# Delta rule: half of the state products and of the next key product between the levels, and a first copy of every second column

## The reference, cut to what matters

```
A   = -beta_t * (K K^T) * decay, below the diagonal      (128 x 128)
T   = (I - A)^-1                                         by doubling, levels 1 to 6
Z   = V - exp(g) * (K S)                                 S: state before the chunk
U   = beta * (T Z)
O   = exp(g) * (Q S)  +  ((Q K^T) * decay) U
S'  = exp(g_end) * S + K^T (U * decay to the end)
```

## Time and profile before

| | us |
|---|---|
| median of 3 runs | 2904.25 |
| the profiled execution | 2905.02 |
| its span | 2902.9 |
| delta stage, first to last level (1459.2 to 1913.0) | 453.8 |
| TensorE busy in that stretch | 444.44 |

### The profile page before, as it was taken

How to read it: one execution, slowest core, us unless ns; L and a number is a source line. 1 busy time by engine, 2 the same in 40 slices (tenths; PEclk the granted TensorE clock), 3 DMA queues, 4 the chain that set the end, 5 groups by cost and what they waited for, 6 DMA issues and landing times.

```text
span 2902.9 us, 43802 instructions
## 1 busy us (share of the span) xinstructions
PE 2729.6 (94%) x16708; PEld 2265.2 (78%) x16708; DVE 1647.1 (57%) x2847; ACT 1177.6 (41%) x2145; POOL 370.2 (13%) x583
## 2 busy tenths in 40 slices
PE   6999899998898997999999999999999998988899
PEld 4756777777757996887688888877777787977899
DVE  4565533334665666885377777773433345468565
ACT  4343422223534445346344455552422234343443
POOL 0000000000000000000066666640000000023000
PEclk9999999999999998999999999999999999999999
DMA  7263244442363553223200000032444433210453
GB/s 281 87 248 130 88 188 159 173 160 86 121 229 132 177 185 144 89 102 109 94 1 1 1 1 1 1 117 87 152 172 170 171 116 127 73 59 15 150 184 144
DMA packets 49614, 343.36 MB, mean 118 GB/s; under 512 B 5296, under 2 KB 7344, under 8 KB 9776
## 3 DMA queue, kind: packets, MB, share of 16 engines
q1 hardware_dynamic: 44960, 324.03, 30.1%
q10 hardware_dynamic: 4496, 17.15, 1.5%
HBM read 333.82 MB, written 7.34 MB: 118 GB/s over the span
## 4 chain that ended last, share of the span: by engine, by line
PE 85%; DVE 8%; ACT 4%; issue 2%; DMA 2%; POOL 0%; DVEq 0%; ACTq 0%; SPq 0%; PEldq 0%; PEld 0%; POOLq 0%
PE ps L558 20%; PE ps L560 20%; PE ps L559 20%; PE ps L2030 4%; PE ps L2017 3%; PE ps L764 3%; PE ps L2009 2%; PE ps L2038 2%; DMA ring<-in_w_dram 2%; PE ps L819 1%; DVE ring_rest L546 1%; ACT H L532 1%; PE ps L1986 1%; PE ps L1972 1%; PE ps L794 1%
## 5 line engine op out<-in xcount | busy, mean ns | idle before, releaser
L558 PE MATMUL ps<-hidden_high,w_high 128*128 128x256 f32 (+1 forms) x1160 | 389.2, 336 | 8.9 <-DVE h_rest L554 6.1
L1130 ACT ACTIVATE w_high<-ring 128x2048 fp32r<-128x2048 f32 x124 | 237.0, 1911 | 381.3 <-DMA ring<-in_w_dram 258.9
L558 PE MATMUL ps<-h_high,w_high 128*128 128x512 f32 (+1 forms) x1024 | 351.2, 343 | 16.4 <-DVE h_low L1553 13.6
L559 PE MATMUL ps<-h_low,w_high 128*128 128x512 f32 (+1 forms) x1024 | 348.0, 340 | 0.0
L559 PE MATMUL ps<-hidden_low,w_high 128*128 128x512 f32 (+1 forms) x1024 | 343.5, 335 | 0.0
L1562 DVE TENSOR_TENSOR mix_high<-ring,w_high 128x2048 fp32r<-128x2048 f32 x56 | 128.4, 2293 | 245.1 <-ACT w_high L1130 245.1
L560 PE MATMUL ps<-hidden_high,ring_rest 128*128 128x256 f32 (+1 forms) x872 | 265.1, 304 | 0.0
L2351 POOL TENSOR_SCALAR RS<-C,arena 128x128 f32<-128x128 f32 x128 | 74.9, 603 | 1444.2 <-DVEq L1932 1444.2
L558 PEld LDWEIGHTS ps<-hidden_high,w_high 128*128 128x128 f32 x1160 | 218.3, 188 | 42.5 <-issue 16.5
L558 PEld LDWEIGHTS ps<-h_high,w_high 128*128 128x128 f32 x1024 | 196.1, 192 | 44.8 <-issue 24.8
L1562 DVE TENSOR_TENSOR ring_rest<-ring,w_high 128x2048 fp32r<-128x2048 f32 x68 | 155.9, 2293 | 123.3 <-ACT w_high L1130 123.3
(11 more groups left out here) (445 smaller groups left out, 6112.2 us busy)
## 6 DMA issues: line engine op xcount, KB each, us to landing
ring<-in_w_dram SPq DMA_DIRECT2D x302, 1024.0 KB, 4.8
z_spill<-arena ACTq DMA_DIRECT2D x16, 256.0 KB, 2.0
arena<-z_spill SPq DMA_DIRECT2D x2, 2048.0 KB, 9.6
C<-in_first_dram ACTq DMA_DIRECT2D x1, 2432.0 KB, 12.2
X<-in_x_dram ACTq DMA_DIRECT2D x1, 2048.0 KB, 13.1
x_spill<-X ACTq DMA_DIRECT2D x1, 2048.0 KB, 6.4
X<-x_spill SPq DMA_DIRECT2D x1, 2048.0 KB, 7.6
C<-in_third_dram ACTq DMA_DIRECT2D x1, 2048.0 KB, 10.1
```

The source lines that it names most:

```text
L558: ins = nc.tensor.matmul(out_, w_high, high, start=first, stop=False)
L559: nc.tensor.matmul(out_, w_high, rest, start=False, stop=False)
L1130: nc.scalar.activation(W_HIGH[:, (j + 1) % 2, :], ring[:, s], ACT.Copy).then_inc(sems["w_high"], 1)
```

## The change

One of the two 128x256 matmuls of `queries_of_state`, of `keys_of_state` and of the next pass's `qk`, for each unit, moves out of the tail and to a place behind product H of a level: queries X behind level 1, queries H behind 2, keys X behind 3, keys H behind 4, the next pass's `qk` X behind 5 and H behind 6. `after_gate` X of the next pass moves from level 6 to behind product H of level 5. Two of the four output multiplications a unit (h = 2, 3) move on VectorE from the tail to between `mask_y` H and `move` X of levels 2 to 5; they read their product from bank 4u+3. The predicated copy of `first_level` takes only the columns of one parity. The counts in the semaphore waits follow.

```diff
-            def qk(i, u):
+            def qk(i, u, h):
                 pe.wait_ge(sems[f"keys{u}"], 2 * (i + 1))
                 if i:
-                    pe.wait_ge(sems[f"y_masked{u}"], LEVELS * i)
-                for h in range(2):
-                    ins = nc.tensor.matmul(ps[:, 4 * u + 3, h * 256:(h + 1) * 256], ...
+                    pe.wait_ge(sems[f"y_masked{u}"], LEVELS * i - (1 - u if h else 0))
+                nc.tensor.matmul(ps[:, 4 * u + 3, h * 256:(h + 1) * 256], ...
...
+            def keys_of_state(i, u, h, n):
+                pe.wait_ge(sems[f"x_kept{u}"], LEVELS * i + n)
+                of_state(i, u, h, 0, 4 * u, "zs")
+            def queries_beside_y(i, u, n):
+                pe.wait_ge(sems[f"y_masked{u}"], LEVELS * i + n)
+                of_state(i, u, 1, 1, 4 * u + 3, "os")
             def queries_of_state(i, u):
                 pe.wait_ge(sems[f"moved{u}"], LEVELS * (i + 1))
-                of_state(i, u, 1, 4 * u + 1, "os")
+                of_state(i, u, 0, 1, 4 * u + 1, "os")
+            def between(i, n):
+                if n < 3:
+                    queries_beside_y(i, n - 1, n)
+                elif n < 5:
+                    keys_of_state(i, n - 3, 1, n)
+                elif i < LAST:
+                    if n == 5:
+                        after_gate(i + 1, 0)
+                    qk(i + 1, n - 5, 1)
...
-                    for u in range(2):
-                        if n == 6 and i < LAST:
-                            after_gate(i + 1, u)
+                    if n == 6 and i < LAST:
+                        after_gate(i + 1, 1)
                     for u in range(2):
                         product(i, n, u)
+                    between(i, n)
...
-                nc.vector.copy_predicated(tt_of(u, 1).rearrange("p (t q l) -> p q t l", t=2, l=2), sides(mask, 1), sides(unit(u, PTT), 1)).then_inc(sems[f"ti{u}"], 1)
+                odd = 1 - PASSES[i][0]
+                to = tt_of(u, 1).rearrange("p (t q l) -> p q t l", t=2, l=2)
+                nc.vector.copy_predicated(to[:, :, :, odd:odd + 1], sides(mask, 1)[:, :, :, odd:odd + 1],
+                                          sides(unit(u, PTT), 1)[:, :, :, odd:odd + 1]).then_inc(sems[f"ti{u}"], 1)
...
+            def output_beside_y(i, n):
+                u, h = (n - 2) // 2, 2 + n % 2
+                dve.wait_ge(sems[f"os{u}"], 2 * i + 1)
...
+                output_of(i, u, h, 4 * u + 3)
...
                     for u in range(2):
                         mask_y(i, n, u)
+                    if 1 < n < 6:
+                        output_beside_y(i, n)
                     for u in range(2):
                         move(i, n, u)
```

More of the change, by code:

```diff
@@ L1979, in turn_keys @@
                 ins.then_inc(sems[f"keys_turned{u}"], 1)
-            def qk(i, u):
+            def qk(i, u, h):
                 pe.wait_ge(sems[f"keys{u}"], 2 * (i + 1))
                 if i:
-                    pe.wait_ge(sems[f"y_masked{u}"], LEVELS * i)
-                for h in range(2):
-                    ins = nc.tensor.matmul(ps[:, 4 * u + 3, h * 256:(h + 1) * 256], key_heads(i, u)[:, h, 0:P], key_heads(i, u)[:, h, :], start=True, stop=True)
-                ins.then_inc(sems[f"qk{u}"], 1)
+                    pe.wait_ge(sems[f"y_masked{u}"], LEVELS * i - (1 - u if h else 0))
+                nc.tensor.matmul(ps[:, 4 * u + 3, h * 256:(h + 1) * 256], key_heads(i, u)[:, h, 0:P], key_heads(i, u)[:, h, :],
+                                 start=True, stop=True).then_inc(sems[f"qk{u}"], 1)
             def turn_first(i, u):
@@ L2032, in product, with of_state @@
                 ins.then_inc(sems[f"product{u}"], 1)
[L2034 to L2043, removed]
+            def of_state(i, u, h, part_, b, name):
+                S = SS[:, bass.ds(PASSES[i][2] * 8 + (4 * u + 2 * h), 2), :]
+                nc.tensor.matmul(ps[:, b, h * 256:(h + 1) * 256], key_heads(i, u)[:, h, part_ * P:(part_ + 1) * P], S,
+                                 start=True, stop=True).then_inc(sems[f"{name}{u}"], 1)
+            def keys_of_state(i, u, h, n):
[4 more added lines that the diff above has]
+                of_state(i, u, 1, 1, 4 * u + 3, "os")
             def queries_of_state(i, u):
                 pe.wait_ge(sems[f"moved{u}"], LEVELS * (i + 1))
-                of_state(i, u, 1, 4 * u + 1, "os")
+                of_state(i, u, 0, 1, 4 * u + 1, "os")
[8 more added lines that the diff above has]
+                    qk(i + 1, n - 5, 1)
             def solve(i, u):
@@ L2081, in pe_delta @@
             for u in range(2):
-                qk(0, u)
+                for h in range(2):
+                    qk(0, u, h)
             for u in range(2):
@@ L2089, in pe_delta @@
                         sides_of(i, n, u)
[L2090 to L2092 removed]
+                    if n == 6 and i < LAST:
+                        after_gate(i + 1, 1)
                     for u in range(2):
                         product(i, n, u)
+                    between(i, n)
                 for u in range(2):
[L2096 removed]
+                    keys_of_state(i, u, 0, LEVELS)
                 for u in range(2):
                     if i < LAST:
[L2099 removed]
+                        qk(i + 1, u, 0)
                     solve(i, u)
@@ L2127, in keep_q @@
             def keep_q(i, u):
-                act.wait_ge(sems[f"qk{u}"], i + 1)
+                act.wait_ge(sems[f"qk{u}"], 2 * (i + 1))
                 if u == 1:
@@ L2235, in first @@
                 dve.wait_ge(sems[f"decay{u}"], i + 1)
-                dve.wait_ge(sems[f"qk{u}"], i + 1)
+                dve.wait_ge(sems[f"qk{u}"], 2 * (i + 1))
                 if u == 0:
@@ L2270, in value_rest @@
                 d, c, hp = PASSES[i]
-                dve.wait_ge(sems[f"zs{u}"], i + 1)
+                dve.wait_ge(sems[f"zs{u}"], 2 * (i + 1))
                 for h in range(4):
@@ L2276, in value_rest, with output_of @@
                 ins.then_inc(sems[f"z{u}"], 1)
-            def state_output(i, u):
[L2279 to L2290, removed]
+            def output_of(i, u, h, b):
+                d, c, hp = PASSES[i]
+                hs = slice(h * P, (h + 1) * P)
+                oo = OO[:, bass.ds(hp * 8 + (4 * u + h), 1), bass.ds(c * P, P)].rearrange("p a b -> p (a b)")
+                if d == 0:
+                    return nc.vector.tensor_scalar(oo, ps[:, b, hs], col(SEG, d, c, hp, u, h), None, ALU.mult)
+                return nc.vector.scalar_tensor_tensor(oo, ps[:, b, hs], col(SEG, d, c, hp, u, h), oo, ALU.mult, ALU.add)
+            def output_beside_y(i, n):
+                u, h = (n - 2) // 2, 2 + n % 2
+                dve.wait_ge(sems[f"os{u}"], 2 * i + 1)
+                if i == 0 and n == 2:
+                    for m in range(3):
+                        dve.wait_ge(sems[f"z_out{m}"], 16 * len(range(m, ZTILES, 3)))
+                output_of(i, u, h, 4 * u + 3)
+            def state_output(i, u):
+                dve.wait_ge(sems[f"os{u}"], 2 * (i + 1))
+                for h in range(2):
+                    ins = output_of(i, u, h, 4 * u + 1)
                 ins.then_inc(sems[f"o{u}"], 1)
@@ L2301, in next_state @@
                 else:
-                    dve.wait_ge(sems[f"os{u}"], i + 1)
+                    dve.wait_ge(sems[f"os{u}"], 2 * (i + 1))
                     ins = nc.vector.memset(SS[:, four(u, hp), :], 0.0)
@@ L2356, in keys @@
                 if i > 1:
-                    pool.wait_ge(sems[f"os{u}"], i - 1)
+                    pool.wait_ge(sems[f"os{u}"], 2 * (i - 1))
                 for part_, t0 in ((0, 8), (1, 0)):
```

## The result

The changed kernel takes 2915.45 us (median of 8 runs, 2910.72 to 2916.53), the one before 2903.66 (8 runs, 2900.68 to 2905.38): ratio 1.0037, 95% interval 1.0027 to 1.0048. It is slower, by about 11 us. The forecast was 2911 with a range of 2902 to 2918.

A forecast was written before the change was run, and what follows sets the result against it. TensorE, busy 94% of the span, bounds the kernel. Twelve passes with state at +0.67 us (+8.0), three without (-0.8) and the last (0) give +7.2: 2912.2, less 0.8 for the median, say 2911 us; range 2902 to 2918.

The forecast's parts named there:

- Inner levels: Levels 2 to 4: each takes 3.01 us in place of 2.65 with the added matmul, +1.08 a pass.
- Level 5 and 6: Level 5 becomes 3.87 us (+1.22); level 6 to its L2030 X becomes 2.19 (-0.92).
- Tail with state: Tail of 12 passes: 12.09 us for 12.69, gaining 0.60, not 2.15, because ScalarE is next.
- Tail without state: Three passes keeping no state: L2009 X at 10.12 us, tail -1.93, whole pass -0.28, together -0.8.
- I take 0.7: Predicated copy in the tail: half the elements take 0.7 us, for 1.40 with all 512.
- The other end of my bound: Three passes without state: with an unshortened copy of 1.4 us, each gains 0.45 us less.
- gets about as much back: Last pass: pays 1.08 us in its levels and regains about that in its end, sum 0.
- my own case: Whole execution: 2911 us plus or minus 3, from the summed terms, chance 0.60.
- the fourth rival: Tail gives nothing: VectorE is last again or the output multiplication delays move X; 2918 us, chance 0.12.
- The first two rivals: Matmuls fit into the levels' pause, 2889 us, chance 0.05; TensorE bounds the tail, all 2.15 comes, 2892.5, chance 0.06.
- the third: Tail gives 0.9 to 1.2 us as ScalarE and VectorE pieces start earlier; 2906 us, chance 0.17.
- the 0.9 that I had named as a sign of being wrong: Level 1: the prediction is wrong if mask X starts later than 0.9 us after L2009 X.

The follow-up runs named there:

- between_products: Changed kernel with the moved matmuls of levels 1, 3, 4 and 5 issued between product X and product H; ratio to before 1.0015, stage 456.5 us.
- gate_back: Changed kernel with the decay exponent (after_gate) of unit X back in level 6; ratio to before 1.0042, stage 464.3 us.
- after_long: Changed kernel with its predicated copy of every second column looped over 128 columns innermost; ratio to before 1.0034, stage 463.0 us.
- long_copy: Kernel before with the predicated copy of every second column, looped over 128 columns innermost; ratio 0.9973, stage 444.2 us.
- copy_only: Kernel before with only the new predicated copy of every second column, loop order unchanged; ratio 1.0007, stage 453.7 us.
- qk_late: Changed kernel with the level 6 half of the next key product of H issued behind the keys-of-state products and the other half; ratio to before 1.0024, stage 459.9 us.

## Why the prediction was right, and what it missed

- **Inner levels, 3.01 in place of 2.65.** Levels 2 to 4 are right to the hundredth in every one of the 16 passes. The gap in front of L2009 X, 0.02 us, decided it, and between_products shows that the place was the cost.
- **Level 5 and 6, 3.87 and 2.19.** Right in all 15 passes that have a next one; gate_back shows the exponent's move is neutral.
- **Tail with state, 12.09; measured 12.16.** ScalarE was next, as said: scale_u H started at 6.67, the time forecast, took 2.23 for 2.17, and turn_first H came at 9.05 for 8.94. With the rest, a pass costs +0.71 us for the predicted 0.67 (tail -0.53, level 1 -0.14, level 6 -0.92, levels 2 to 4 +1.08, level 5 +1.22): 12 x 0.71 = 8.5, predicted 8.0.
- **Tail without state, 10.12; measured 10.52.** The step that failed here is the copy, "I take 0.7": it took 1.30. The other end of my bound, 0.45 more, is what came, and after_long, with 0.73, measured 10.08. So such a pass cost 0.12 us where it was to give 0.28: the three together +0.4 for the predicted -0.8.
- **The first pass** was left out of the sum. Its level 1 (3.10 before) isn't held by VectorE, which is idle for 0.2 us before mask X, and L2009 X behind it starts as soon as product H is issued, so there was no gap to close: the matmul of 0.43 was added in full, 3.54: +0.4 us.
- **The last pass "gets about as much back".** This step failed. TensorE had its transposes of the next stage (L2503) 1.1 us earlier behind the last L2009 X, but that stage then waited for others:

```profile
1936.68 0.63 PE L2503 MATMUL ps<-ident,arena 128*128 128x128 f32 x4 [0.46 <-POOL arena L2454]
1936.72 1.41 DVE L2487 SCALAR_TENSOR_TENSOR arena<-ps,V,arena 128x512 f32<-128x512 f32 x2 [1.01 <-DMA arena<-z_spill]
```

VectorE waits 1.01 us for the transfer that brings z back. The next stage's first product (L558) still comes 0.4 us earlier (17.6 us behind the last L2009 X for 18.0), but the end of the span doesn't: it lies 989.9 us behind the last L2009 X in both traces. In the executions with the same granted clock in that part (0.975) it is 989.5 and 990.2 with the end of the kernel before (long_copy, copy_only) and 989.6 to 989.9 with that of the changed one. So the 1.1 us in the levels of this pass came back nowhere. Where in that part the 0.4 goes is open; no run tested it.

Together, passes with state, passes without, first and last: 8.5 + 0.4 + 0.4 + 1.1 = 10.4 of the stage's 10.6, for 8.0 - 0.8 + 0 + 0 = 7.2 predicted.

So the mechanism was right where most of the time is, in the levels and in the 12 tails with state. The number was helped by a wide range: the growth is about half again as large as forecast, the misses all point the same way, and 2915.45 lies above my own case (2911 plus or minus 3), near the 2918 of the fourth rival, whose mechanism did not come.

The first two rivals fell: the levels did not hide the matmuls (3.01, not 2.65) and TensorE did not bound the tail (0.62 of wait before turn_first H, and qk_late). Of the third, no extra gain of 0.3 or more came. Of the fourth neither part came: the tail gave 0.53, move X was ready 0.47 before its use, and mask X of level 1 started 0.88 after L2009 X in the 12 passes behind one with state. It started later than the 0.9 that I had named as a sign of being wrong in the first pass (1.22) and behind the three passes without state (1.02); in these three level 1 took 3.01 all the same. The two waits of TensorE in the tail, 0.45 and 0.62 us, are 1.07 together for the 1.3 of the prediction. Copying every second column, the last part of the change, gained nothing (copy_only).

Beside the 262 cycles the prediction cites a sustained rate from the same section of the Trainium skill, "TensorE: Matmul & The Clock Gate". That rate is given there for 128 and 512 columns only, not for the 256 of this kernel; no term of the sum used it.

## What to carry to other kernels

An engine with pauses has room only where the pauses are: read them from the starts of its instructions, not from its busy share, and put added work in front of an instruction that waits. Behind the last instruction of the level a matmul of 0.43 us cost 0.36 here, in front of one that waited 0.14. Work taken out of a saturated stretch gives back only down to the next chain; lay that chain out before moving anything. And where a strided instruction is slow, try the other order of its loops before fewer elements: here one statement was worth 9.1 us of the stage, the two moves that paid another 4.

## What the runs showed of the hardware

The predicated copy's time follows neither its elements nor its rows. In each unit it writes the same tile, all elements have 4 bytes, and the times are medians of the 16 copies of a trace: 512 elements with the result alternating between two halves every 2 elements 1.40 us (unit H 1.31); 256 elements alternating every element 1.29 to 1.41; 512 written straight on, sources in pairs 4 columns apart 0.73 (unit X 0.84); 256 with result every 2nd and sources every 4th column 0.73 (unit X in long_copy 0.84); 512 so strided 1.43 (measured in unit X only, whose copies ran about 0.1 longer than those of H in the kernels on the base of before; why is open). The Trainium skill, "SBUF — State Buffer", section "Specifications (TRN2)", says that SBUF goes by lines of 16 bytes (four fp32 columns), needs two hits on a line for full bandwidth, and charges each step to a new line. The two strided forms agree with it: sources with one hit a line cost about twice per element (512 in 1.43, 256 in 0.73) what pairs cost (512 in 0.73). The alternating result isn't explained by it: it has two hits a line and a new line for every pair, as the sources of the 0.73 form have, and took 1.40. No run here separates the jump between the halves from the line, or a result from a source.

A wait of TensorE costs more than its length: the four instructions after it took 0.68 in place of 0.61, some 0.07 us a stop. That is how an added matmul that closes a gap can cost less than itself: behind a level of the earlier trace rows it took away the gap of 0.02 and the restart of L2009 X (a row of 0.44 before, 0.38 after), so 0.43 cost 0.36.
